# Down projection of a two-layer trunk: 16 of 22 inner tiles by a seven-product scheme, and three reorders

## The chip, the cores and the metric

The kernel runs on one core of a Trainium2 chip. What counts is the device time of one execution in microseconds (us); a measured version is given as the median of its executions, and the profile is of one execution taken by itself.

## The reference

One step of a streaming encoder: 1024 prompt tokens and 32 sample tokens, 1056 in all (`T`), with a model width of 1024, through two layers. Layer 0 mixes tokens by gated linear attention, layer 1 by latent attention with 8 heads; each layer ends with the same channel mixer, which is what most of the change is about:

```python
def conv_glu(h, prev, w_in, conv_w, conv_b, w_out):
    g, u = jnp.split(h @ w_in, [D_FF], axis=-1)
    gc, new_prev = causal_dwconv(g, prev, conv_w, conv_b)
    return (jax.nn.gelu(gc, approximate=False) * u) @ w_out, new_prev
...
x = x + o
h = rmsnorm(x, norm_ffn[l])
o, prev = conv_glu(h, ffn_prev0[l], w_ffn_in[l], ffn_conv_w[l], ffn_conv_b[l], w_ffn_out[l])
x = x + o
```

`D_FF` is 2816, the causal convolution has three taps, and everything is float32.

## The kernel before

**Precision.** Each float32 product of matrices is made of three products of rounded numbers: a factor is split into a rounded part (`hi`, an ACT copy to `F32R`) and the rest (`lo`, a subtraction on DVE or POOL), and the products hi by hi, lo by hi and hi by lo are summed in PSUM. The lines are 341 to 343 (`mm3`) for plain products and 758 to 760 (`product`) for the seven-product scheme. Every operand that PE uses thus costs an ACT copy and a subtraction first.

**Layout.** Features lie on the 128 partitions. The residual stream `xT` is 8 tiles of 128 features by 1056 tokens. The inner width 2816 is 22 tiles of 128 (`NF`). All large loads and stores are issued by SP on one hardware queue (`wraw`, two slots for weights; `s_a`, `s_x`, DRAM scratch).

**First half of the mixer, `pe_unit_ffn`.** For each inner tile the gate rows and the up rows are to be computed for all tokens: a 2 by 2 problem (gate and up rows; left and right 528 tokens; lower and upper half of the 1024 features). Tile 0 is done plainly, the tiles 1 to 21 (called units here) with seven products in place of eight: P1 P2 P6 P5 P7 P4 P3. A product is 4 pieces of 128 features by 3 matmuls by 2 halves of 264 columns, 24 matmuls; a unit is 168 matmuls. The sums that the scheme needs are made of weights by `s_sums` (DVE, four subtractions or additions of 128x512) and of activations once per layer by `t_sum` (T1 to T4). PSUM results leave through ACT copies (`snap`, three in a unit) and DVE additions of 128x528 (`gate_left`, `up_right`, `up_left`, `gate_right`). Then DVE runs the convolution (`conv`, lines 1076 to 1093), ACT the GELU (`gelu`), DVE the product with the up rows (`glu`), and SP stores the tile to `s_a` (`sp_a_out`).

**Second half, `pe_down_first` and `pe_down_ffn`.** 11 groups of 2 inner tiles. A group multiplies 2 by 128 rows of `w_ffn_out` with its two activation tiles for 8 output tiles and 3 chunks of 352 tokens: 8 x 3 x 2 x 3 = 144 matmuls of 352 columns. DVE adds each of the 24 results of 128x352 to `xT` (L585; in the first group L1153, which reads the residual stream back through `xback`). For each group SP reloads two `s_a` tiles (`sp_a_in`), ACT rounds them (L935, L939) and POOL makes the rest (L1193, L1195).

**What sets the order.** Nothing is scheduled by a program: each engine has its own list, written out by hand (`pe_ffn`, `act_ffn`, `dve_ffn`, `pool_ffn`, `sp_ffn`), and waits on counting semaphores where another engine's result or a free buffer is needed. An instruction that waits holds back everything behind it on its engine. SP's list at the end of the units is driven by PE's product counter `prod`: one load or store after each product.

**The other places.** For the second tile, `snap(2, 0)` copies P1 into the gate buffer `fg[0]`, which `conv(0)` still reads, so ACT waits for the convolution of tile 0:

```python
                if n == 0:
                    act.wait_ge(S("row_zeros"), layer + 1)
                    act.wait_ge(S("conv"), NF * layer + f - 1)
                    state_in(f)
```

In the latent attention, `head_split(act, 0)` (L2405) rounds the first head's keys `akraw`, after a load has brought them, and stands in ACT's list right behind the rounding of the last keys and ahead of the copies of the last query tiles (L2080, L2085). In the attention steps, DVE adds two blocks of the output projection to `xT` in each step (`add(s, 0)` and `add(s, 1)`, L585); the second stands behind the reciprocal and the scaling of the softmax rows (L2507, L2509).

## Time and profile before

| | |
|---|---|
| median of 3 executions | 2638.41 us (2638.26 to 2638.42) |
| the profiled execution, its own time | 2640.56 us |
| its span, first to last instruction | 2638.7 us |
| PE busy | 2579.3 us (98%) |
| DVE / ACT / POOL busy | 1487.2 / 1000.7 / 932.6 us (56 / 38 / 35%) |
| mean granted TensorE clock | 0.995 |
| DMA | 221.93 MB, mean 84 GB/s |

The span is 1.9 us shorter than the profiled execution's own time, and that is 2.1 us above the median. PE is the matmul engine; its busy time includes the overlapping tails of matmuls, so what a matmul costs is read from the distance between two starts. "Idle before" in a row is the time in which an engine waited before that instruction, and the arrow names what ended the wait.

### The profile page before, as it was taken

What the parts mean: (1) busy time and instruction counts of PE and PEld (TensorE: products, weight loads), DVE (VectorE), ACT (ScalarE), POOL (GpSimd) and SP (SyncE); (2) the same over time, 40 slices, a digit from 0 to 9 for tenths busy, and PEclk for the clock granted to TensorE, in tenths of its full rate; (3) what the DMA queues carried; (4) which work ended last, traced back from release to release, by engine and by line L of the source; (5) the groups of instructions that cost most, each with busy time, mean ns of one, the idle gap of its engine ahead of it and who ended that gap; (6) DMA issues with size and microseconds to landing.
All of it is one profiled execution on the core that took longest, in us unless ns stands there. A gap on an engine that the chain in (4) does not pass through costs nothing.

```text
span 2638.7 us, 43372 instructions
## 1 busy us (share of the span) xinstructions
PE 2579.3 (98%) x18206; PEld 2500.3 (95%) x18206; DVE 1487.2 (56%) x2660; ACT 1000.7 (38%) x1651; POOL 932.6 (35%) x546
## 2 busy tenths in 40 slices
PE   8999999999999999999999989999999999999999
PEld 7999999999999999999998988889999999999999
DVE  6735353578555455555625875555696555446554
ACT  6333333364233322111547756444453233321111
POOL 5121212152433444444522223223334433444441
PEclk9999999999999999999999999999999999999999
DMA  3111111122222224222213253132122222233222
GB/s 110 35 37 35 37 39 34 38 98 81 81 74 90 74 81 180 74 98 98 70 45 126 108 198 124 49 98 73 61 71 82 81 73 89 74 136 117 98 98 100
DMA packets 182159, 221.93 MB, mean 84 GB/s; under 512 B 16690, under 2 KB 145344, under 8 KB 181328
## 3 DMA queue, kind: packets, MB, share of 16 engines
q1 hardware_dynamic: 179567, 217.08, 24.5%
q8 instruction: 144, 2.36, 0.4%
q10 hardware_dynamic: 2400, 2.10, 0.3%
q14 instruction: 48, 0.39, 0.0%
HBM read 160.56 MB, written 58.59 MB: 83 GB/s over the span
## 4 chain that ended last, share of the span: by engine, by line
PE 89%; DVE 6%; ACT 2%; issue 1%; DMA 1%; SPq 0%; POOL 0%; DVEq 0%; ACTq 0%; POOLq 0%
PE ps L341 14%; PE ps L343 13%; PE ps L342 13%; PE ps L758 11%; PE ps L760 11%; PE ps L759 11%; PE ps L2366 3%; PE ps L1289 1%; PE ps L2350 1%; PE ps L1276 1%; PE ps L1277 1%; PE ps L1278 1%; DVE xT L585 1%; PE ps L1365 1%; PE ps L1348 1%
## 5 line engine op out<-in xcount | busy, mean ns | idle before, releaser
L585 DVE TENSOR_TENSOR xT<-xT,ps 128x352 f32<-128x352 f32 x672 | 347.2, 519 | 249.2 <-PE ps L343 248.1
L1170 POOL TENSOR_TENSOR wlo<-wraw,whi 128x1024 fp32r<-128x1024 f32 x78 | 187.3, 2401 | 454.7 <-DVE s_raw L993 454.7
L306 POOL TENSOR_TENSOR wlo<-wraw,whi 128x2048 fp32r<-128x2048 f32 (+1 forms) x37 | 168.3, 4550 | 498.2 <-ACT whi L299 468.8
L341 PE MATMUL ps<-fahi,whi 128*128 128x352 f32 x960 | 311.1, 324 | 0.1
L343 PE MATMUL ps<-fahi,wlo 128*128 128x352 f32 x960 | 308.1, 321 | 0.0
L342 PE MATMUL ps<-falo,whi 128*128 128x352 f32 x960 | 307.9, 321 | 0.0
L299 ACT ACTIVATE whi<-wraw 128x2048 fp32r<-128x2048 f32 x40 | 76.6, 1914 | 396.7 <-DMA wraw<-w_ffn_out 328.1
L341 PE MATMUL ps<-hh,whi 128*128 128x352 f32 x648 | 218.5, 337 | 0.6 <-ACT cqr L2679 0.3
L343 PE MATMUL ps<-hh,wlo 128*128 128x352 f32 x648 | 208.2, 321 | 0.0
L342 PE MATMUL ps<-hl,whi 128*128 128x352 f32 x648 | 207.9, 321 | 0.0
L758 PE MATMUL ps<-hh,whi 128*128 128x264 f32 x672 | 191.5, 285 | 0.4 <-DVE wlo L1019 0.4
L759 PE MATMUL ps<-hl,whi 128*128 128x264 f32 x672 | 191.2, 285 | 0.0
L760 PE MATMUL ps<-hh,wlo 128*128 128x264 f32 x672 | 191.2, 284 | 0.0
L341 PEld LDWEIGHTS ps<-fahi,whi 128*128 128x128 f32 x960 | 180.1, 188 | 0.9 <-DVE xT L585 0.4
L342 PEld LDWEIGHTS ps<-falo,whi 128*128 128x128 f32 x960 | 180.4, 188 | 0.2
L343 PEld LDWEIGHTS ps<-fahi,wlo 128*128 128x128 f32 x960 | 180.3, 188 | 0.0
L1170 POOL TENSOR_TENSOR s_lo<-s_raw,s_hi 128x512 fp32r<-128x512 f32 x80 | 148.4, 1855 | 60.0 <-ACT s_hi L890 60.0
L1047 DVE TENSOR_TENSOR hf<-hf,ps 128x528 f32<-128x528 f32 x42 | 29.6, 704 | 188.6 <-ACT hf L926 188.6
L758 PEld LDWEIGHTS ps<-hh,whi 128*128 128x128 f32 x672 | 126.5, 188 | 1.3 <-DVE wlo L1019 0.8
L341 PEld LDWEIGHTS ps<-hh,whi 128*128 128x128 f32 x648 | 121.6, 188 | 5.7 <-issue 2.6
L760 PEld LDWEIGHTS ps<-hh,wlo 128*128 128x128 f32 x672 | 126.6, 188 | 0.0
L759 PEld LDWEIGHTS ps<-hl,whi 128*128 128x128 f32 x672 | 126.4, 188 | 0.0
(414 smaller groups left out, 7920.0 us busy)
## 6 DMA issues: line engine op xcount, KB each, us to landing
wraw<-w_ffn_in SPq DMA_DIRECT2D x88, 512.0 KB, 3.8
s_a<-hf SPq DMA_DIRECT2D x44, 528.0 KB, 3.3
wraw<-w_ffn_out SPq DMA_DIRECT2D x44, 512.0 KB, 4.3
fa<-s_a SPq DMA_DIRECT2D x40, 528.0 KB, 6.1
...
```

The costliest lines, as they stand in the source:

```text
L299: act.activation(hi[:, 0:cols], raw[:, 0:cols], ACT.Copy).then_inc(S("w_hi"), 1)
L306: pool.tensor_tensor(lo[:, 0:cols], raw[:, 0:cols], hi[:, 0:cols].bitcast(F32), ALU.subtract).then_inc(S("w_lo"), 1)
L341: nc.tensor.matmul(out, w[0], x[0], start=start, stop=False)
L342: nc.tensor.matmul(out, w[0], x[1], start=False, stop=False)
L343: return nc.tensor.matmul(out, w[1], x[0], start=False, stop=stop)
L585: dve.tensor_tensor(xT[:, m, tc(j)], xT[:, m, tc(j)], ps[:, banks[i % len(banks)], 0:TC], ALU.add)\
L758: nc.tensor.matmul(out, w_[0], x_[0], start=first, stop=False, skip_group_check=True)
L759: nc.tensor.matmul(out, w_[0], x_[1], start=False, stop=False, skip_group_check=True)
L760: last = nc.tensor.matmul(out, w_[1], x_[0], start=False, stop=(k == HK - 1), skip_group_check=True)
L1047: dve.tensor_tensor(right, left, two(U_SIDE), ALU.add).then_inc(S("summed"), 1)
L1170: return pool.tensor_tensor(lo[:, cols], raw[:, cols], hi[:, cols].bitcast(F32), ALU.subtract)
L2366: last = pe.matmul(ps[:, 6, 0:m], av[h % 2][0:n, kk0 // P, :], aPT[s % 2][0:n, i, 0:m], start=(i == 0), stop=(i == len(tiles) - 1))
```

## The change

The down projection of the inner tiles 1 to 16 moves to the seven-product scheme. Two parts of 8 inner tiles, four pairs of output tiles in each: `ND` = 8 more units per layer (numbers 22 to 29, `pe_unit_down`), each again 7 products of 24 matmuls of 264 columns. The 2 by 2 problem is now: two output tiles of a pair; odd and even inner tiles (X11 and X21 on the left 528 tokens, X22 on the right); left and right tokens. The six inner tiles that are left (0, 17 to 21) make `NG2` = 3 groups of the old kind.

What comes with it: the activation sums T1 to T4 are made tile pair by tile pair on DVE while the units 3 to 17 run (`pair_sum`, four of 128x528 in each odd unit), stored to a new scratch `s_t` (`sp_t_out`, 8 stores of 1.08 MB), and reloaded in blocks of 1.08 MB, seven for each part (`sp_block`), which ACT rounds (`block_hi`, 128x2112) and DVE (five of seven) or POOL (T3 and X22) splits (`block_lo`). The weights of a unit are a 512 KB load for each of two halves (`sp_down_w`); their sums S2, S3, S4 go into space freed in other buffers (`side`), S4 of an even unit into the rows of the last even activation tile and of an odd unit into those of the last odd one, so the sum waits for that tile's store. `into_x` adds PSUM results of 128x528 to `xT`, seven in a unit; `xT` is reloaded from `s_x` in four loads of 1.08 MB (`sp_x_in`).

The three reorders: `snap(2, 0)` goes to a buffer of its own (`first_left`), and the wait on the first convolution moves to `snap(2, 1)` and `gate_left(2)`; `head_split(act, 0)` moves behind the copies of the last query tiles; in steps with 32 rows (`STEPS[s][1] == NG`) the second addition to `xT` comes before the reciprocal.

The core of the diff:

```diff
+ND = 8
...
+        first_left = h32[:, 0, TH:T]
...
+        PAIRS = ((3, 4), (0, 1), (2, 5), (6, 7))
...
+        def side(n, f):
+
+            cols = slice(TH, TH + QB)
+            if n == "S3" and f % 2:
+                return fcr[:, QB:2 * QB], fc[:, 0:QB], fcr[:, 0:QB]
+            if n == "S4":
+                at_ = (2 * (f % 2) + 1) * T + TH
+                return hh[:, 2 * (f % 2), cols], hf32[:, at_:at_ + QB], hh[:, 2 * (f % 2) + 1, cols]
+            r_ = 0 if n == "S2" else 2
+            return hl[:, r_, cols], h32[:, r_ + 1, cols], hl[:, r_ + 1, cols]
+
...
+        def sp_block(sp, layer, part, i):
+
+            name, n = BLOCKS[part][i], 7 * part + i
+            if A_LOADS * layer + n >= 2:
+                before, count = load_count(layer, n - 2)
+                sp.wait_ge(S(before), nth(before, count))
+            if name[0] == "T":
+                sp.wait_ge(S("t_stored"), nth("t_stored", 16 * (NT * layer + 4 * part + 4)))
+                src = A["s_t"][4 * part:4 * part + 4, :, ("T1", "T3", "T2", "T4").index(name), :].rearrange("q p t -> p q t")
+            else:
+                odd = name == "X11"
+                sp.wait_ge(S(f"a_stored{int(odd)}"), nth(f"a_stored{int(odd)}", 16 * (NFG * layer + 4 * part + 4 + (not odd))))
+                first, t0 = ND * part + (1 if odd else 2), TH if name == "X22" else 0
+                src = A["s_a"][first:first + ND - 1:2, :, t0:t0 + TH].rearrange("q p t -> p q t")
+            sem, _ = load_count(layer, n)
+            sp.dma_start(xblock(name)[1], src).then_inc(S(sem), 16)
...
+        def sp_x_in(sp, layer, p):
+
+            sem = f"x_back{p % 2}"
+            if p >= 2:
+                sp.wait_ge(S(sem), nth(sem, 16 * (2 * layer + 1)))
+            m0, m1 = PAIRS[p]
+            rows = slice(m0, m1 + 1, m1 - m0)
+            sp.dma_start(xT[:, rows, :], A["s_x"][:, rows, :]).then_inc(S(sem), 16)
...
-            sp_a_in(sp, layer, 0)
+            sp_block(sp, layer, 0, 0)
+            prod(f, 2)
+            sp_block(sp, layer, 0, 1)
+            sp_next_w(sp, layer, c0, f + 2, 0)
+            sp_x_in(sp, layer, 0)
             prod(f, 3)
-            sp.dma_start(xback[0][:, :, :], A["s_x"][:, 0:HK, :]).then_inc(S("x_back0"), 16)
+            sp_block(sp, layer, 0, 2)
             sp_a_out(sp, layer, f - 1)
-            prod(f, 4)
-            sp_a_in(sp, layer, 1)
-            prod(f, 5)
-            sp.dma_start(xback[1][:, :, :], A["s_x"][:, HK:KD, :]).then_inc(S("x_back1"), 16)
-            prod(f, 6)
-            sp_w_out(sp, layer, c0, 1)
+            for n in (4, 5, 6):
+                prod(f, n)
+                sp_block(sp, layer, 0, n - 1)
+            sp_next_w(sp, layer, c0, f + 2, 1)
+            prod(f, 7)
+            sp_block(sp, layer, 0, 6)
+            sp_x_in(sp, layer, 1)
+            sp.wait_ge(S("conv"), NF * layer + NF - 1)
+            sp_x_in(sp, layer, 2)
+            for f in range(NF, NF + ND):
+                last = f == NF + ND - 1
+                for n in range(1, 8):
+                    if n in (2, 7) or f == NF + 3 or last and n in (3, 4):
+                        prod(f, n)
+                    if f == NF + 3:
+                        sp_block(sp, layer, 1, n - 1)
+                    if last and n in (3, 4):
+                        sp_a_in(sp, layer, n - 3)
+                    if n in (2, 7):
+                        sp_next_w(sp, layer, c0, f + 2, n // 7)
+                if f == NF:
+                    sp.wait_ge(S("conv"), NF * (layer + 1))
+                    sp_x_in(sp, layer, 3)
+                    sp_a_out(sp, layer, NF - 1)
             sp_a_in(sp, layer, 2)
-            sp_a_out(sp, layer, f)
-            for g in range(2, NFG):
-                sp.wait_ge(S("down_mm"), 24 * (b0 + g - 1))
-                sp_w_out(sp, layer, c0, g)
-                if g > 2:
-                    sp_a_in(sp, layer, g)
+            sp.wait_ge(S("down_mm"), 24 * (b0 + 1))
+            for kk in range(2):
+                sp_w_out(sp, layer, c0, 2, kk)
...
+            def p7():
+                low_pool(1)
+                pe.wait_ge(S("s_lo"), cnt("s_lo", layer, f, 3))
+                pe.wait_ge(S("summed"), cnt("summed", layer, f, 3))
+                product(a, w_extra("S3"), x_in("T3"), True).then_inc(S("prod"), 1)
+
+            def p3():
+                low_pool(2)
+                pe.wait_ge(S("s_lo"), cnt("s_lo", layer, f, 4))
+                pe.wait_ge(S("summed"), cnt("summed", layer, f, 4))
+                product(U_SIDE, w_extra("S4"), x_in("X22"), True).then_inc(S("prod"), 1)
...
+                act.wait_ge(S("prod"), cnt("prod", layer, f, ORDER(f).index(("P1", "P6", "P7")[n]) + 1))
+                if n == (1 if f == 2 else 0):
...
+                if (f, n) == (2, 0):
+                    dst = first_left
...
+            def refill(part, f, early, late):
+
+                block_hi(part, 0)
+                early()
+                block_hi(part, 1)
+                side_hi(f, "S2")
+                late()
+                block_hi(part, 2)
+                block_hi(part, 3)
+                w_hi_side(f)
+                block_hi(part, 4)
+                side_hi(f, "S3")
+                side_hi(f, "S4")
+                block_hi(part, 5)
+                block_hi(part, 6)
...
+                if f in (NF, NF + 1):
+                    stored = f"a_stored{f % 2}"
+                    dve.wait_ge(S(stored), nth(stored, 16 * NFG * (layer + 1)))
                 dve.tensor_tensor(s4, w[1], s2, ALU.subtract).then_inc(S("s_sum"), 1)
...
+                if f == NF - 1:
+                    w_low_in(f + 1)
+                    block_lo(0, 0)
+                    block_lo(0, 1)
+                pair = (f - 3) // 2 if f % 2 and f <= 2 * NT + 1 else None
+                if pair is not None:
+                    pair_sum(pair, "T1")
+                    pair_sum(pair, "T3")
+                up_right(f)
+                if f == NF - 1:
...
+            for f in range(NF, NF + ND):
+                part, first, more = (f - NF) // 4, (f - NF) % 4 == 0, f + 1 < NF + ND
+                side_lo(f, "S2")
+                if first:
+                    into_x(f, 1)
+                    block_lo(part, 3)
+                w_low_side(f)
+                if not first:
+                    into_x(f, 1)
+                side_lo(f, "S3")
+                if f == NF:
+                    conv(NF - 1)
+                into_x(f, 2)
+                if f > NF:
+                    side_lo(f, "S4")
+                into_x(f, 3)
+                if f == NF:
+                    side_lo(f, "S4")
+                if first:
+                    into_x(f, 4)
+                    block_lo(part, BLOCKS[part].index("T4"))
+                    if f == NF:
+                        glu(NF - 1)
+                    into_x(f, 5)
                     s_sums(f + 1)
-                up_right(f)
-                up_left(f)
-                gate_right(f)
-                conv(f)
-
-            before = 24 * b0
...
+            for part in range(2):
+                for name in ("T3", "X22"):
+                    block_lo(part, name)
...
+                early = s < NS and STEPS[s][1] == NG
+                if early:
+                    add(s, 1)
...
-                if PREP[u] == (MP - 1, "ks", 1, 3):
+                if PREP[u] == (MP - 1, "q", 0, 2):
                     head_split(act, 0)
-                if PREP[u] == (MP - 1, "q", 0, 2):
                     q_split(act, 0)
```

**First place, SP's queue at the end of the units** (layer 0). Before, from the reload of the first group's tiles (`h_52<-s_a`) on; the number behind a name is that of the buffer, and `z_mm` is the name of the counter that `prod` uses, `x_loaded0` and `x_loaded1` those of the stores of even and odd tiles:

```order
L668 DMA h_52<-s_a 128x2x528 [waits x_loaded1,x_loaded0,z_mm]
L668 DMA h_52<-s_a 128x2x528
L717 DMA xback_130<-s_x 128x4224 [waits z_mm]
L661 DMA s_a<-hf_219 256x1x528 [waits glu]
L671 DMA fa_137<-s_a 128x1056 [waits x_loaded1,x_loaded0,z_mm]
L671 DMA fa_137<-s_a 128x1056
L722 DMA xback_131<-s_x 128x4224 [waits z_mm]
```

Now, from the first block (X11) to the store of tile 21:

```order
L741 DMA h_52<-s_a 128x4x528 [waits x_loaded1,z_mm]
L741 DMA h_52<-s_a 128x4x528 [waits x_loaded0,z_mm]
L332 DMA wraw_55<-w_ffn_out 128x8x128
L759 DMA xT<-s_x 128x2112
L741 DMA hflat<-s_t 128x4x528 [waits consts,x_loaded2,z_mm]
L720 DMA s_a<-hf_220 256x1x528 [waits glu]
...
L332 DMA wraw_56<-w_ffn_out 128x8x128 [waits z_mm] x2
L759 DMA xT<-s_x 128x2112 [waits consts_late,conv]
L720 DMA s_a<-hf_220 256x1x528 [waits glu]
```

The store of tile 20 (the first `s_a<-hf_220`) has four loads ahead of it that were not there, and that of tile 21 (the last row) follows a weight load and a load of `xT`.

**Second place, DVE in unit 21** (layer 0). Before:

```order
L1042 TENSOR_TENSOR fg_111<-fg_111,ps 128x528 [waits z_mm,z_ln]
L1101 TENSOR_TENSOR hf_219<-hf_219,fc 128x2x528 [waits gelu]
L1047 TENSOR_TENSOR hf_219<-hf_219,ps 128x528 [waits z_ln]
L1053 TENSOR_TENSOR hf_219<-hf_219,ps 128x528 [waits z_min,z_mm]
L1065 TENSOR_TENSOR fg_111<-fg_111,ps 128x528 [waits z_mm]
```

Now:

```order
L1266 TENSOR_TENSOR fg_111<-fg_111,ps 128x528 [waits z_mm,z_ln]
L1325 TENSOR_TENSOR hf_220<-hf_220,fc 128x2x528 [waits gelu]
L1192 TENSOR_TENSOR h_52<-wraw_56 128x512 [waits consts,w_loaded1]
L1194 TENSOR_TENSOR wraw_56<-wraw_56 128x4x128 [waits z_scan]
L1196 TENSOR_TENSOR h_52<-wraw_56 128x512 [waits z_scan]
L1201 TENSOR_TENSOR hf_220<-wraw_56,h_52 128x512 [waits x_loaded0,z_scan]
L1242 TENSOR_TENSOR wlo_58<-wraw_56,whi_54 128x1024 [waits z_scan,w_hi]
L1331 TENSOR_TENSOR hl<-h_52,hh 128x4x528 [waits b_exp] x2
L1271 TENSOR_TENSOR hf_220<-hf_220,ps 128x528 [waits z_ln]
L1331 TENSOR_TENSOR T2lo<-hflat,T2hi 128x2112 [waits b_exp]
```

Between the product with the up rows (L1325) and `up_right(21)` (L1271), for which PE's last product waits, there are now the four weight sums of unit 22, the last with the wait on the store of tile 20, and three subtractions.

**Third place, ACT ahead of the attention**, before:

```order
L2096 ACTIVATE ksq<-ksq 128x1568 [waits unit_act]
L2405 ACTIVATE akh_181<-akraw_185 128x1568 [waits head_loaded0]
L2080 ACTIVATE qw<-ps 128x352 [waits q_left,normed,unit_mm]
L2085 ACTIVATE sqh_164<-ps 128x352 [waits unit_mm]
L2080 ACTIVATE qw<-ps 128x352 [waits unit_mm]
```

Now:

```order
L2403 ACTIVATE ksq<-ksq 128x1568 [waits unit_act]
L2387 ACTIVATE qw<-ps 128x352 [waits q_left,normed,unit_mm]
L2392 ACTIVATE sqh_166<-ps 128x352 [waits unit_mm]
...
L2392 ACTIVATE sqh_166<-ps 128x352 [waits unit_mm]
L2712 ACTIVATE akh_183<-akraw_187 128x1568 [waits head_loaded0]
```

The rounding of the keys, with its wait on a load, moved from ahead of six PSUM copies to behind them.

## Rows read from the trace of the kernel before

**Rows 1.** The page's busy times over the whole span

```profile
PE 2579.3 (98%) x18206; PEld 2500.3 (95%) x18206; DVE 1487.2 (56%) x2660; ACT 1000.7 (38%) x1651; POOL 932.6 (35%) x546
```

**Rows 2.** Windows: length, busy (instructions) of the five engines, clock, DMA share, GB/s

```profile
700.00:800.00 100.00, 100.00 (x825) 100.00 (x824) 52.03 (x85) 32.02 (x40) 39.74 (x20) 1.00 0.25 81
```

**Rows 3.** By source line: ns minimum/median/maximum, first and last start (groups 1 and 2 for PE)

```profile
L1065 DVE TENSOR_TENSOR fg<-fg,ps x19: 704/705/706, 662.2 to 1029.6; 128x528 f32<-128x528 f32 x19
...
L342 PE MATMUL ps<-falo,whi x48: 318/322/324, 1052.6 to 1075.0; 128*128 128x352 f32 x48
...
L341 PE MATMUL ps<-hhf,whi x48: 321/323/326, 1029.4 to 1052.0; 128*128 128x352 f32 x48
```

**Rows 4.** By source line: the sums, roundings and splits that the change repeats

```profile
L989 DVE TENSOR_TENSOR wraw<-wraw 128x512 f32<-128x512 f32 x15 | 10.4, 693 | 0.5
...
L1015 DVE TENSOR_TENSOR T2lo<-hflat,T2hi x2: 2345/2347/2349, 599.8 to 1944.6; 128x2112 fp32r<-128x2112 f32 x2
...
L1019 DVE TENSOR_TENSOR wlo<-wraw,whi x2: 1218/1222/1226, 602.1 to 613.6; 128x1024 fp32r<-128x1024 f32 x2
...
L935 ACT ACTIVATE hhf<-h x2: 1959/1959/1959, 1018.5 to 2363.3; 128x2112 fp32r<-128x2112 f32 x2
...
L1195 POOL TENSOR_TENSOR falo<-fa,fahi x10: 4742/4760/4781, 1045.7 to 1247.6; 128x2112 fp32r<-128x2112 f32 x10
```

**Rows 5.** SP's timeline, the landing times of stores (L661), and a window

```profile
1017.97 0.34 SPq L717 DMA_DIRECT2D xback<-s_x  x1
1018.35 0.56 SPq L661 DMA_DIRECT2D s_a<-hf  x1
...
DMA to landing us min/median/max: 3.1/3.3/9.3
...
1030.00:1040.00 10.00, 10.00 (x65) 10.00 (x64) 9.66 (x20) 1.97 (x2) 0.00 (x0) 1.00 1.00 416
```

**Rows 6.** Timelines of DVE and POOL: start, duration, instruction, wait before

```profile
619.43 3.27 DVE L1083 SCALAR_TENSOR_TENSOR fc<-fg,par,fc 128x1024 f32<-128x1024 f32 x1
...
640.76 1.28 DVE L1083 SCALAR_TENSOR_TENSOR fc<-fg,par,fc 128x1024 f32<-128x1024 f32 x1
...
658.16 0.70 DVE L1047 TENSOR_TENSOR hf<-hf,ps 128x528 f32<-128x528 f32 x1 [3.00 <-ACT hf L926]
...
618.79 2.83 POOL L1170 TENSOR_TENSOR s_lo<-s_raw,s_hi 128x1024 fp32r<-128x1024 f32 x1
...
657.66 1.30 POOL L1170 TENSOR_TENSOR s_lo<-s_raw,s_hi 128x512 fp32r<-128x512 f32 x1
```

**Rows 7.** PE's waits: total us, times, longest us

```profile
PE ps L341 <- DVE xT L585: 10.4, 25, 1.3
PE ps L758 <- ACT fg L926: 8.6, 2, 4.3
```

**Rows 8.** Timelines of PE and ACT at unit 2, and a window

```profile
625.33 0.56 PE L758 MATMUL ps<-T2hi,s_hi 128*128 128x264 f32 x1 [4.32 <-ACT fg L926]
...
629.60 0.29 PE L758 MATMUL ps<-T1hi,whi 128*128 128x264 f32 x1
...
624.59 0.59 ACT L926 ACTIVATE fg<-ps 128x528 f32<-128x528 f32 x1
...
625.00:630.00 5.00, 4.67 (x28) 4.70 (x29) 3.06 (x4) 3.70 (x5) 0.00 (x0) 0.69 0.01 3
```

**Rows 9.** Timelines of ACT and PE ahead of the attention

```profile
1559.17 1.51 ACT L2405 ACTIVATE akh<-akraw 128x1568 fp32r<-128x1568 f32 x1 [4.77 <-DMA apraw<-s_p]
...
1563.55 0.63 PE L2050 MATMUL ps<-sqh,ones_r 128*128 128x352 f32 x1 [5.03 <-DVE qsl L2109]
```

**Rows 10.** Timelines of DVE and PE at a step with 32 rows

```profile
1667.25 0.70 DVE L2509 TENSOR_SCALAR aP<-aP,rl 32x544 f32<-32x544 f32 x1
1667.88 0.50 DVE L585 TENSOR_TENSOR xT<-xT,ps 128x352 f32<-128x352 f32 x1
...
1668.44 0.43 PE L341 MATMUL ps<-oh,moh 128*128 128x352 f32 x1 [0.87 <-DVE xT L585]
```

More of the change, by code:

```diff
@@ L763, in pe_unit_ffn @@
         def pe_unit_ffn(pe, layer, c, f):
-            u = unit_no(layer, f)
             slot = c[0]
@@ new lines, in s_sums @@
+                s2, s3, s4 = [v.rearrange("p (k n) -> p k n", k=HK) for v in (
+                    [raw[:, n * QB:(n + 1) * QB] for n in range(3)] if f < NF else
+                    [side(n, f)[1] for n in ("S2", "S3", "S4")])]
+                dve.wait_ge(S(f"w_loaded{slot}"), 32 * loads)
+                if 2 < f < NF:
+                    dve.wait_ge(S("prod"), cnt("prod", layer, f - 1, 0))
+                if f == NF:
+                    dve.wait_ge(S("t_stored"), nth("t_stored", 16 * NT * (layer + 1)))
@@ L2510, in dve_att @@
                                       None, ALU.mult).then_inc(S("probs"), 1)
-                add(s, 1)
+                if not early:
+                    add(s, 1)
             down_norm_dve(dve, fill_before(MP - 1), 3, 3, R_FFN + KD,
```

459 lines of the change are left out of this document (300 added, 159 removed).

## Prediction, written before the run

> **What bounds the kernel now.** I read the busy times first, then windows, the waits of PE, and timelines where PE waits. PE is busy 98% of the span [rows 1]. In a window of the units PE has 825 matmuls in 100 us without a gap at clock 1.00, while DVE is busy 52%, POOL 40%, ACT 32% and the DMA share is 0.25 [rows 2]: there matmul time is the bound, and the other engines have room on average. PE waits little, most for additions to `xT` (10.4 us in 25 waits) and for ACT's copy `fg` (8.6 us in 2) [rows 7]. So what saves matmuls shortens the kernel, and what makes PE wait lengthens it in full. All sums below are against the profiled execution (2640.6); the median is 2.2 lower, which I take off at the end.
>
> **The change, part by part.**
>
> *1. Matmuls.* The last addition of a unit (L1065) starts at 662.2 the first time and at 1029.6 the nineteenth: 18 periods, 20.41 us each [rows 3], so 121.5 ns for each of 168 matmuls and 2.915 us for a product. In the first down group the 48 matmuls of L341 start from 1029.4 to 1052.0, 47 steps in 22.6, so the group takes 23.1; in the second L342 gives 47 steps in 22.4, 22.9 [rows 3]. I take 23.0 for a group of 144, 159.7 ns for a matmul. A group and a unit replace each other one for one, eight per layer: 8 x (23.0 - 20.41) = 20.7, **-41 us** for both layers (ends: 22.9 and 23.1, -40 and -43).
>
> *2. Pair sums* (four additions of 128x528 in each odd unit). One costs 0.70 to 0.72 by the row of such an addition [rows 3]. DVE has 48% idle in the units [rows 2]; T1 and T3 end before `up_right` is needed by PE's next product but one, and the convolution ends 1.6 later, still ahead of the next snapshot. Cost 0; the upper bound is 1 us in each of 16 units if POOL holds them up. The stores to `s_t` are 8 x 1.08 MB beside a DMA share of 0.25: 0.
>
> *3. First refill (units 21 to 23), the largest term.* I worked out the timeline of all engines step by step from their lists. t = 0 is the start of unit 21's first product; product n of it ends at 2.915 n.
> What SP's queue does: a store alone lands in 3.3 us; the one issued 0.4 behind a load of 2.16 MB lands in 9.3 [rows 5]. At 0.41 MB per us (416 GB/s at a DMA share of 1.00, rows 5) the 0.54 MB of a store are 1.3, so some 1.9 are fixed. Served in order of issue, load and store end 1.9 + 2.70/0.41 = 8.5 after the load's issue; measured are 9.7. So the store does stand behind the load, and the 1.2 more go to the upper end. The Trainium skill ("DMA: Bandwidth & Descriptors", Queues, rings and completion order) also says that each DMA engine consumes descriptors in ring order; by that rule, the trace agrees.
> (a) The store of tile 20 is issued at t = 9.5, after product 3. Ahead of it in the queue stand block 1, a weight half (0.52 MB), a load of `xT` (1.08) and block 2; block 0, issued at 3.2, is through at 7.7. So 7.7 + (1.08 + 0.52 + 1.08 + 1.08 + 0.54)/0.41 = 18.2, with the completion 18.6. On DVE the fourth sum of unit 22 waits for it. Behind it stand that sum 0.7, a split of 1024 1.2, two splits of 2112 at 2.35 each [rows 4], and only then `up_right(21)` 0.7: 18.6 + 7.3 = 25.9. PE wants it for the seventh product at 17.5: **8.5 us**.
> (b) Unit 22: P7 waits for the `xT` addition behind the last convolution (1.5), and POOL's two splits of 4.76 [rows 4] hold DVE's (P3 1.8, P4 1.2): **4.5 us**.
> (c) The store of tile 21 is issued behind unit 22's last product, a weight half and the last load of `xT`: 1.9 + 2.14/0.41 and some issue time = 7.2 after the product's end; then a sum 0.7, an addition 0.7, a split 1.2, and only then P1 of unit 23: **10 us**.
> The blocking used in (b): L1083 took 3.27 at 619.43 while POOL ran 618.79 to 621.62, against 1.28 alone, and an addition out of PSUM ran in its usual 0.70 beside a POOL instruction [rows 6]. So POOL holds up DVE instructions with two SBUF operands, not those with PSUM.
> (d) Clock: after a stall of 4.32 us the product took 625.33 to 629.60 = 4.27 in place of 2.915, with granted clock 0.69 in 625:630 [rows 8]: part of it ran at the lower level (1.2 GHz). I add 1.4 to 1.7 for each of the stalls (a), (c): **3.2**.
>
> *4. Second refill (unit 26).* Loads start three products early and are in time. DVE's split of the fourth block and `side_lo` wait behind POOL's T3 and X22: P6 2.4 and P5 4.6, with the clock 1.5 more: **8.5 us**. If POOL didn't hold DVE, 0.
>
> *5. Units 23 to 25, 27 to 29, three groups.* About 20 DVE instructions of 0.6 to 1.2, some 15 us in 20.4: hidden, 0 to 0.2.
> Sum of 3 to 5: 8.5 + 4.5 + 10 + 3.2 + 8.5 + 0.2 = 35 per layer; with a DMA rate of 0.39 it is 36.4. I take 36, **+72**. Ends: 33 and 40 per layer.
>
> *6. Second tile's snapshot.* PE waits 4.32 us at 625.33, and 8.6 in both layers [rows 7, 8], plus 1.4 each of clock. P6 could begin at 620.85. But P7 then waits for `snap(2, 1)`, which stands behind the convolution and a GELU (0.6). And the weight sums of unit 3 stand on DVE behind the first product with the up rows and start as before, so POOL's splits do too, and DVE's second convolution, held by them (its long step at 640.76, rows 6), moves little; `up_left(2)` stands behind it, and P2 of unit 3 waits for that. I get P2 of unit 3 some 1.7 earlier per layer. **-3.4**; ends 0 and -11.4 (2 x 5.7).
>
> *7. First keys.* ACT's L2405 waited 4.77 us for a load, the query copies behind it came late, and PE idled 5.03 at 1563.55 [rows 9]. Moved: the copies start when PE has their sums, 4 to 5 earlier. L2405 takes 1.51 behind six copies of 0.45, and POOL's split of the keys follows it; the first scores need that only some 15 us later, which covers it. Nothing else is queued behind it that PE needs sooner. **-5.5** with the clock; ends 0 and -6.7.
>
> *8. Rows of 32.* The addition at 1667.88 stands behind a scaling of 0.70, and PE waits 0.87 at 1668.44 [rows 10]; three such waits of about 0.9. **-2.5**; ends 0 and -3.
>
> **Sum.** 2640.6 - 41 + 72 - 3.4 - 5.5 - 2.5 = 2660.2; less 2.2: **2658 us**, 0.7% slower.
>
> **A rule that weighs on 3(b) and 4.** The rows show a DVE instruction held until POOL's was over [rows 6], in one order only: POOL had begun first. The Trainium skill ("SBUF — State Buffer", Who interferes with whom) says that whichever starts first keeps the shared ports for its whole instruction. By it, POOL's splits are held by DVE's as well, where DVE is first; that moves T3 and X22 later and would cost up to 2 us more per layer, 2662 in place of 2658. No row here shows POOL held.
>
> **The rivals.** A measurement of this kernel can tell about 0.2% (5.3 us) from no change.
>
> *A, POOL doesn't hold DVE in the refills* (the splits alternate, DVE finds gaps). Then 3(b) is 1.5 and 4 is 0: 25 per layer, 2588.2 + 50 - 2.2 = **2636**, no change. Against: rows 6. Chance 0.13.
>
> *B, the stores are not behind the loads* (land 3.3 after issue). (a) becomes 2.5, (c) 7.1, part of it returns as waits in unit 22: 29 per layer, **2644**. Against: 9.3 in rows 5. Chance 0.08.
>
> *C, the other side: DVE is in time.* At P3 of unit 21 and P1 of unit 23 PE finds what it needs nearly ready, since stores land as if alone and no DVE instruction is held. What is left is 13 per layer, the time by which the stores are issued late: 2588.2 + 26 - 2.2 = **2612**, 1% faster. It decides from stalls under 23.5 us per layer (2588.2 + 47 - 2.2 = 2633). For it: engines other than PE are half idle [rows 2]. Against: both rows named above. I also leave room for steps that I read too strictly. Chance 0.19.
>
> *D, more waits than I count*: loads of 1.08 MB with rows of 2112 bytes slower than 0.41 MB per us, POOL held too, the keys' reorder worth nothing: 40 per layer and +5.5, **2672**. Chance 0.10.
>
> **Numbers.** Forecast 0.50, own range 2648 to 2668 (ends of 3 and 6 to 8). Faster by over 0.2%: C and a third of A, 0.24. Within: most of A, half of B, 0.12. Slower: 0.64. The range of 8 in 10 reaches up to D's value and down into C: 2618 to 2672.
>
> **What would show it.** Right: PE waiting about 8 us ahead of P3 of unit 21 and about 10 ahead of P1 of unit 23 in each layer, with the clock below 0.9 behind both; the stores of tiles 20 and 21 landing 7 to 9 us after issue; waits of 2 to 5 in unit 26 with DVE instructions stretched beside POOL's of 4.7; matmuls in units 22 to 29 121.5 ns apart; PE's wait at unit 2 under 1; no 5.03 ahead of the query sums. Wrong: total PE waits in the refills under 23 us per layer (then C), stretches without stall but units over 20.5 us (then DVE bounds them).

## The result, and the profile after

The changed kernel takes 2676.40 us (median of 4, 2675.4 to 2678.53) against 2638.41 before: ratio 1.0144, 95% interval 1.0128 to 1.0159, so 38 us slower. The forecast was slower, but by 20 us, and its range ended at 2672. The profiled execution took 2675.52 with a span of 2673.4, so the profile shows 34.7 us of the 38.

The first rows of the page, and the clock from the view of the cores:

```profile
span 2673.4 us, 44342 instructions
PE 2556.9 (96%) x18590; PEld 2477.3 (93%) x18590; DVE 1657.6 (62%) x2616; ACT 1051.2 (39%) x1727; POOL 842.1 (31%) x522
core 0: 2673.4 us, clock 0.983
```

Against [rows 1] PE is busy 22 us less, although the kernel is longer: there are 384 matmuls more, but shorter ones; matmul time was saved, and waits took its place. PE's waits, as total, times, longest:

```profile
PE ps L864 <- DVE wlo L1242: 29.4, 7, 11.3
PE ps L864 <- DVE hf L1271: 22.4, 4, 10.3
PE ps L864 <- DVE xT L1351: 16.0, 4, 5.8
...
PE ps L864 <- DVE hf L1277: 5.0, 2, 2.5
PE ps L345 <- DVE xT L589: 7.2, 19, 1.3
PE ps L345 <- POOL apl L2264: 3.9, 1, 3.9
```

L864 is the first matmul line of a product. The three first rows were not there before: the weight split of the next unit (`w_low_in`), `up_right(21)` and the additions to `xT`. Of the 8.6 us behind `fg` 0.7 are left, and 3.2 of the 10.4 behind `xT` are gone [rows 7], but a wait for `up_left(2)` (L1277) and one for POOL's last split for the first scores (`apl`) are new.

Where the 34.7 us of span are, by distances between the same instructions in both traces:

| stretch | before | after | difference | on record |
|---|---|---|---|---|
| last addition of unit 1 to that of unit 20, both layers | 787.4 | 784.9 | -2.5 | -3.4 |
| unit 20's last addition to the last group's last L341/L345, layer 0 | 275.4 | 299.0 | +23.6 | +15.3 |
| the same, layer 1 | 277.6 | 300.7 | +23.1 | +15.3 |
| last root of the keys to the first scaled step of 768 | 42.4 | 37.0 | -5.4 | -5.5 |
| from there to the last such step | 280.7 | 277.2 | -3.5 | -2.5 |
| all else (from the unrounded distances) | | | -0.5 | 0 |

The pairs of units with and without pair sums take 21.1 and 19.7 us by their last additions, 40.8 together, twice 20.41 [rows 3]: the pair sums are hidden. So the down projection costs 46.7 us where 30.6 were forecast, and the reorders give 11.5 where 11.4 were.

Inside a layer, unit 20's last addition to the first matmul of the groups takes 227.2 us (1006.55 to 1233.73); nine units of 20.41 are 183.7. So 43.5 are lost. PE's timeline (start, duration, matmul, wait before) has five long waits in layer 0, and the same five in layer 1 within 0.1 (the products behind them within 0.3):

```profile
1034.29 0.59 PE L864 MATMUL ps<-hh,s_hi 128*128 128x264 f32 x1 [10.27 <-DVE hf L1271]
...
1057.04 0.56 PE L864 MATMUL ps<-T3hi,hl 128*128 128x264 f32 x1 [5.78 <-DVE xT L1351]
...
1080.02 0.59 PE L864 MATMUL ps<-hh,whi 128*128 128x264 f32 x1 [11.34 <-DVE wlo L1242]
...
1154.83 0.37 PE L864 MATMUL ps<-T1hi,whi 128*128 128x264 f32 x1 [2.97 <-DVE wlo L1242]
...
1161.76 0.46 PE L864 MATMUL ps<-T3hi,hl 128*128 128x264 f32 x1 [2.24 <-DVE xT L1351]
```

| place | wait forecast | wait measured | its product's 24 matmuls over 2.915 us |
|---|---|---|---|
| P3 of unit 21 | 8.5 | 10.3 | 2.2 |
| unit 22: P7 | 1.5 | 5.8 | 2.5 |
| unit 22: P3, P4 | 3.0 | under 0.25 | 0.2, 0.2 |
| P1 of unit 23 | 10 | 11.3 | 1.6 |
| unit 26: P6 | 2.4 | under 0.25 | 0.2 |
| unit 26: P5, P7 | 4.6 | 3.0, 2.2 | 1.8, 1.6 |
| sum | 30 | 32.6 | 10.3 (forecast 4.7) |

The waits come to 32.6 us and the slow products to 10.3, 9.7 of it right behind the five waits; together 42.9 of the 43.5. In windows behind the first, second and third wait the clock (the seventh number, after the busy times) is at its lower level, or for part of the window (0.67):

```profile
1034.00:1037.00 3.00, 2.71 (x12) 2.71 (x13) 3.00 (x3) 3.00 (x4) 2.49 (x1) 0.50 0.72 214
1037.00:1040.00 3.00, 3.00 (x19) 3.00 (x18) 0.51 (x2) 0.33 (x1) 3.00 (x1) 0.67 0.00 0
1057.00:1060.00 3.00, 2.96 (x13) 2.99 (x14) 3.00 (x3) 0.73 (x1) 0.00 (x0) 0.50 0.02 5
1060.00:1063.00 3.00, 3.00 (x16) 3.00 (x15) 1.78 (x3) 0.00 (x0) 0.00 (x0) 0.52 0.00 0
1080.00:1083.00 3.00, 2.98 (x13) 2.98 (x14) 2.31 (x3) 0.00 (x0) 0.00 (x0) 0.50 0.00 0
```

0.50 is 1.2 of 2.4 GHz. And the two links of the first wait, DVE's and SP's timelines:

```profile
1015.32 0.36 SPq L741 DMA_DIRECT2D hflat<-s_t  x1
1015.72 0.83 SPq L720 DMA_DIRECT2D s_a<-hf  x1
...
1015.71 0.69 DVE L1196 TENSOR_TENSOR h<-wraw 128x512 f32<-128x512 f32 x1
1027.06 0.69 DVE L1201 TENSOR_TENSOR hf<-wraw,h 128x512 f32<-128x512 f32 x1 [10.67 <-DMA s_a<-hf]
```

The store of tile 20 is issued at 1015.72 and lands 11.2 us later; before, one behind a single load took 9.3, one alone 3.3 [rows 5]. The fourth weight sum waits for it, and behind that sum and three splits `up_right(21)` releases PE.

The wait ahead of P7 of unit 22 has another cause than the last convolution by itself. POOL's and DVE's timelines there:

```profile
1046.97 4.94 POOL L1493 TENSOR_TENSOR hl<-h,hh 128x2112 fp32r<-128x2112 f32 x1 [5.89 <-ACT hh L1106]
...
1047.24 4.72 DVE L1300 COPY sm<-fg 128x32 f32<-128x32 f32 x1
```

The first instruction of that convolution, a copy of 128x32 with a median of 0.18, begins behind POOL's split of X22 and ends with it, 4.5 us late; the rest of the convolution and the addition that P7 waits for follow it. Layer 1 has the same (4.72).

### The profile page after: what moved, and what is told of

The parts are those of the page before. It is cut to its first block, busy times and chain, and to the rows that moved or that the text cites. A ratio compares the mean times of both kernels' runs of the same rounds, so it can differ in the third digit from the quotient of the medians.

```text
span 2673.4 us, 44342 instructions
## 1 busy us (share of the span) xinstructions
PE 2556.9 (96%) x18590; PEld 2477.3 (93%) x18590; DVE 1657.6 (62%) x2616; ACT 1051.2 (39%) x1727; POOL 842.1 (31%) x522
## 4 chain that ended last, share of the span: by engine, by line
PE 82%; DVE 11%; DMA 2%; issue 2%; ACT 2%; POOL 1%; SPq 1%; DVEq 0%; ACTq 0%; POOLq 0%
PE ps L864 14%; PE ps L866 13%; PE ps L865 13%; PE ps L345 9%; PE ps L347 8%; PE ps L346 8%; PE ps L2673 3%; DMA s_a<-hf 1%; PE ps L1596 1%; PE ps L2657 1%; PE ps L1583 1%; PE ps L1585 1%; PE ps L1584 1%; DVE fc L1307 1%; PE ps L2640 1%
## 5 line engine op out<-in xcount | busy, mean ns | idle before, releaser
L864 PE MATMUL ps<-hh,whi 128*128 128x264 f32 x928 | 266.2, 287 | 28.5 <-DVE wlo L1242 23.4
L589 DVE TENSOR_TENSOR xT<-xT,ps 128x352 f32<-128x352 f32 x336 | 172.2, 518 | 106.3 <-PE ps L347 105.2
L345 PE MATMUL ps<-hh,whi 128*128 128x352 f32 x648 | 218.5, 337 | 0.6 <-ACT cqr L2990 0.3
L310 POOL TENSOR_TENSOR wlo<-wraw,whi 128x2048 fp32r<-128x2048 f32 (+1 forms) x21 | 94.3, 4490 | 367.2 <-ACT whi L303 337.9
L864 PEld LDWEIGHTS ps<-hh,whi 128*128 128x128 f32 x928 | 176.0, 190 | 30.0 <-DVE wlo L1242 24.6
L1351 DVE TENSOR_TENSOR xT<-xT,ps 128x528 f32<-128x528 f32 x112 | 78.2, 701 | 109.1 <-PE ps L866 108.9
L864 PE MATMUL ps<-T1hi,whi 128*128 128x264 f32 x464 | 133.6, 288 | 6.0 <-DVE wlo L1242 5.9
L865 PE MATMUL ps<-T1lo,whi 128*128 128x264 f32 x464 | 133.3, 287 | 0.0
L866 PE MATMUL ps<-T1hi,wlo 128*128 128x264 f32 x464 | 133.0, 287 | 0.0
L864 PE MATMUL ps<-T4hi,whi 128*128 128x264 f32 x464 | 132.0, 284 | 0.0
L865 PE MATMUL ps<-T4lo,whi 128*128 128x264 f32 x464 | 131.9, 284 | 0.0
L866 PE MATMUL ps<-T4hi,wlo 128*128 128x264 f32 x464 | 131.5, 283 | 0.0
L345 PEld LDWEIGHTS ps<-hh,whi 128*128 128x128 f32 x648 | 121.6, 188 | 5.6 <-issue 2.6
```

The source lines that it names most:

```text
L310: pool.tensor_tensor(lo[:, 0:cols], raw[:, 0:cols], hi[:, 0:cols].bitcast(F32), ALU.subtract).then_inc(S("w_lo"), 1)
L345: nc.tensor.matmul(out, w[0], x[0], start=start, stop=False)
L589: dve.tensor_tensor(xT[:, m, tc(j)], xT[:, m, tc(j)], ps[:, banks[i % len(banks)], 0:TC], ALU.add)\
L864: nc.tensor.matmul(out, w_[0], x_[0], start=first, stop=False, skip_group_check=True)
L865: nc.tensor.matmul(out, w_[0], x_[1], start=False, stop=False, skip_group_check=True)
L866: last = nc.tensor.matmul(out, w_[1], x_[0], start=False, stop=(k == HK - 1), skip_group_check=True)
```

## The experiments

Two ideas had to be told apart for each wait: the theory (the wait is that of the store or of a DVE instruction that POOL holds up, as on record) and a rival (blocks late anyway, DVE full anyway). The runs were made on several chips, and the kernel before took 2638.4 to 2642.5 on them (the column "before"); all ratios are to it on the same chip. So a difference of times between two rows with different "before" can be off by some 4 us. "Refill" is the distance of 227.2 above, in layers 0 and 1; it is read inside one trace and is the surer measure.

| run | us | before | ratio (95%) | refill, layers 0 and 1 |
|---|---|---|---|---|
| the change | 2676.4 | 2638.4 | 1.0144 (1.0128 to 1.0159) | 227.2, 226.7 |
| e1_store20 | 2666.9 | 2640.0 | 1.0099 (1.0082 to 1.0116) | 223.3, 222.4 |
| e2_store21 | 2647.7 | 2640.0 | 1.0026 (1.0015 to 1.0037) | 213.4, 213.4 |
| e3_both_stores | 2639.6 | 2640.0 | 0.9994 (0.9985 to 1.0004) | 210.6, 209.8 |
| e4_no_pool | 2657.6 | 2640.0 | 1.0071 (1.0053 to 1.0089) | 218.6, 218.3 |
| e5_stores_no_pool | 2618.1 | 2642.5 | 0.9909 (0.9894 to 0.9924) | 198.2, 196.8 |
| e6_reorders_alone | 2626.8 | 2642.5 | 0.9944 (0.9931 to 0.9958) | |
| e7_filler_matmuls | 2674.3 | 2642.5 | 1.0125 (1.0110 to 1.0141) | 226.7, 226.6 |
| e8_store_queue | 2642.0 | 2639.8 | 1.0013 (1.0003 to 1.0023) | 210.8, 210.2 |
| e9_dve_order | 2616.0 | 2639.8 | 0.9907 (0.9891 to 0.9924) | 196.0, 196.5 |
| e10_loads_order | 2612.5 | 2639.8 | 0.9896 (0.9880 to 0.9913) | 193.6, 195.2 |
| e11_keys_alone | 2636.2 | 2640.2 | 0.9982 (0.9972 to 0.9992) |  |
| e12_rows32_alone | 2634.8 | 2640.2 | 0.9979 (0.9969 to 0.9988) |  |

### The stores of tiles 20 and 21

```diff
             sp_block(sp, layer, 0, 1)
+            sp_a_out(sp, layer, f - 1)      # e1, e3
             sp_next_w(sp, layer, c0, f + 2, 0)
             sp_x_in(sp, layer, 0)
             prod(f, 3)
             sp_block(sp, layer, 0, 2)
-            sp_a_out(sp, layer, f - 1)      # e1, e3
...
                 for n in range(1, 8):
+                    if f == NF and n == 3:              # e2, e3
+                        sp_a_out(sp, layer, NF - 1)
...
                     sp_x_in(sp, layer, 3)
-                    sp_a_out(sp, layer, NF - 1)         # e2, e3
```

> The changed kernel with one DMA moved in SP's list: the store of tile 20 is issued before the weight half, the xT load and block 2 instead of behind them. My theory (DVE's fourth weight sum stands behind that store in the queue, and PE's P3 of unit 21 behind DVE): the store lands at about 12.5 us of unit 21 instead of 20.5, PE's wait ahead of P3 falls from 10.3 to about 2 us in each layer, with 1.5 to 2 us of clock, so 2676 - 16 to 20 = 2656 to 2660. Rival (the blocks themselves come too late, the store only happens to be last): the wait falls by under 3 us and the time stays over 2670.

> The changed kernel with the store of tile 21 issued as soon as its product with the up rows is done, ahead of unit 22's last product, the weight half and the xT load. My theory: the 11.3 us ahead of P1 of unit 23 fall to under 1 and the 1.6 us of clock go with them, 12 to 13 us per layer, 2676 - 25 = 2651. Rival (w_low of unit 23 is late for another reason, such as the rounding of the weights on ACT behind a GELU): under 5 us per layer, over 2666.

> Both store moves together. If the two waits are independent: 2676 - 18 - 25 = 2633, within 4 us. If the time saved at the first only moves the wait to the next transfer (X22 and T4 blocks for unit 22), the sum comes out 5 to 12 us short, 2638 to 2645.

DVE in e1_store20, unit 21:

```profile
1017.62 0.69 DVE L1196 TENSOR_TENSOR h<-wraw 128x512 f32<-128x512 f32 x1
1021.07 0.69 DVE L1201 TENSOR_TENSOR hf<-wraw,h 128x512 f32<-128x512 f32 x1 [2.76 <-DMA s_a<-hf]
1021.87 1.23 DVE L1242 TENSOR_TENSOR wlo<-wraw,whi 128x1024 fp32r<-128x1024 f32 x1
1023.01 4.62 DVE L1331 TENSOR_TENSOR hl<-h,hh 128x2112 fp32r<-128x2112 f32 x2
1027.55 0.70 DVE L1271 TENSOR_TENSOR hf<-hf,ps 128x528 f32<-128x528 f32 x1
```

DVE waits 2.8 us for the store in place of 10.7, and PE 2.4 ahead of P3 in place of 10.3, as the theory had it, with the same work between. But only 3.9 of those 8 us stay in the refill: in unit 22 PE now waits 3.4 us ahead of P5, with a slow product of 4.7 behind it, which it didn't before. The cause is in the timelines of POOL and DVE there:

```profile
1037.47 4.95 POOL L1493 TENSOR_TENSOR T3lo<-hflat,T3hi 128x2112 fp32r<-128x2112 f32 x1 [30.34 <-ACT T3hi L1106]
...
1037.79 5.72 DVE L1242 TENSOR_TENSOR wlo<-wraw,whi 128x1024 fp32r<-128x1024 f32 x1
...
1043.61 0.36 PE L864 MATMUL ps<-T1hi,whi 128*128 128x264 f32 x1 [3.36 <-issue]
```

The weight split, 1.22 in the changed kernel, now falls beside POOL's split of T3 and takes 5.72; P5 starts 0.1 after its end. So the wait was given back through the other cause, not through late blocks, and the rival is out. The total is 9.5 us (12 by the ratios), where 16 to 20 were expected.

The second move gave all that it should: the wait of 11.3 is gone, 28.8 us in total (25 expected), 13.8 in the refill. Together they give 36.8 us, of the 38.3 that they give one by one; so the two waits are independent or nearly so. The 2633 expected for that case was missed because the first move gave 9.5 and not 18.

### Is it the queue, or the engines behind it?

```diff
             sp_block(sp, layer, 0, 2)
-            sp_a_out(sp, layer, f - 1)
...
-                    refill(0, f + 1, lambda: snap(NF - 1, 1), lambda: snap(NF - 1, 2))
+                    refill(0, f + 1, lambda: (sp_a_out(act, layer, NF - 2), snap(NF - 1, 1)), lambda: snap(NF - 1, 2))
...
                 w_hi_in(f)
+                if f == NF + 1:
+                    sp_a_out(act, layer, NF - 1)
```

> The changed kernel with the stores of tiles 20 and 21 issued by ACT on its own queue (behind block 0's rounding, and behind the weights of unit 23), all loads left where they are on SP's. If the stores were late because they stood behind loads in one queue, they land 4 to 6 us after their issue though the loads still run, and the waits ahead of P3 of unit 21 and P1 of unit 23 fall to about 2 and 0 to 1: near e3_both_stores, 2640 to 2646. If the DMA engines' load itself makes them late, whatever the queue, they take 7 to 10 us again and the time stays over 2665.

The total is the one of the first expectation, but for half of its reason. Timelines of ACT's queue and DVE:

```profile
1016.06 0.67 ACTq L720 DMA_DIRECT2D s_a<-hf  x1
...
1025.17 0.69 DVE L1201 TENSOR_TENSOR hf<-wraw,h 128x512 f32<-128x512 f32 x1 [7.71 <-DMA s_a<-hf]
...
DMA to landing us min/median/max: 3.1/6.1/9.0
```

The store of tile 20, on a queue of its own and issued at nearly the same time, still takes 9.0 us (11.2 in SP's queue; in layer 1 9.9 and 11.3), and PE waits 7.3. The second, issued when no load runs, takes 3.1, and its wait is gone. So the first is late because loads are in flight on the same engines (a weight half, `xT` rows and T2, 2.7 MB, all issued within 3 us before it or just after); its place in the queue is worth 2 us. What helped in e1_store20 was to issue it before those loads: there it landed after 4.7. The time doesn't tell the two ways apart here: the refill is 210.8 in e8_store_queue and 210.6 in e3_both_stores, where PE waits 2.5 us ahead of P3 but then 3.0 more ahead of P5 of unit 22.

### POOL beside DVE

```diff
-            for part in range(2):
-                for name in ("T3", "X22"):
-                    block_lo(part, name)        # POOL's list
...
                 side_lo(f, "S3")
+                if first:
+                    block_lo(part, 4)           # T3, DVE's list
...
                 if first:
+                    block_lo(part, BLOCKS[part].index("X22"))
                     into_x(f, 4)
```

> The changed kernel with the splits of T3 and X22 made by DVE (2.35 us each) instead of POOL (4.8), so that nothing on POOL runs beside DVE in the refills. My theory (POOL's instruction keeps DVE out): PE's waits in unit 22 (5.8) and unit 26 (3.0 + 2.2) fall to 0 to 2 and the clock losses behind them (2.5, 1.8, 1.6) mostly go, 7 to 12 us per layer: 2652 to 2662. Rival (DVE is simply full in the refills): 4.7 us more work on DVE makes these waits longer by 2 to 5 per layer, 2680 to 2686.

In the changed kernel, POOL and DVE in unit 26:

```profile
1147.35 6.25 POOL L1493 TENSOR_TENSOR T3lo<-hflat,T3hi 128x2112 fp32r<-128x2112 f32 x1 [95.44 <-ACT T3hi L1106]
1153.57 5.67 POOL L1493 TENSOR_TENSOR hl<-h,hh 128x2112 fp32r<-128x2112 f32 x1
...
1146.67 2.35 DVE L1331 TENSOR_TENSOR T1lo<-hflat,T1hi 128x2112 fp32r<-128x2112 f32 x1
1148.94 5.75 DVE L1242 TENSOR_TENSOR wlo<-wraw,whi 128x1024 fp32r<-128x1024 f32 x1
1154.61 5.17 DVE L1336 TENSOR_TENSOR hl<-h,hl 128x512 fp32r<-128x512 f32 x1
```

and DVE in the same unit of e4_no_pool:

```profile
1144.89 2.35 DVE L1332 TENSOR_TENSOR T1lo<-hflat,T1hi 128x2112 fp32r<-128x2112 f32 x1
1147.16 1.22 DVE L1242 TENSOR_TENSOR wlo<-wraw,whi 128x1024 fp32r<-128x1024 f32 x1
1148.30 0.69 DVE L1337 TENSOR_TENSOR hl<-h,hl 128x512 fp32r<-128x512 f32 x1
1148.90 2.35 DVE L1332 TENSOR_TENSOR T3lo<-hflat,T3hi 128x2112 fp32r<-128x2112 f32 x1
```

A split of 1.22 took 5.75, one of 0.69 took 5.17. It goes both ways: POOL's split, 4.76 by itself [rows 4], takes 6.25 when DVE's T1 split has begun 0.7 before it. That is the rule of the Trainium skill that the prediction weighed ("SBUF — State Buffer", Who interferes with whom): here the trace agrees with it in both directions. In e4_no_pool the copy of 128x32 in unit 22 takes 0.18 again too. With 4.7 us more work on DVE, the refill is 8.6 us shorter; in unit 22 the wait ahead of P7 is 3.5, and in unit 26 no wait over 1.2 us is left. The rival is out.

### The clock

```diff
                     if f == NF - 1:
+                        pe.wait_ge(S("snap"), cnt("snap", layer, f, 3))
+                        filler(U_SUM, hh[:, HK, TH:TH + P], hh[:, HK, TH:TH + HH], 76)
                     pe.wait_ge(S("summed"), cnt("summed", layer, f, 2))
...
                 if f == NF + 1:
                     pe.wait_ge(S("snap"), cnt("snap", layer, NF, 0))
+                    filler(a, hh[:, 0, 0:P], hh[:, 0, 0:HH], 86)
                 pe.wait_ge(S("w_lo"), c[1] + 1)
```

> The changed kernel with unused matmuls in the two long waits: 76 ahead of P3 of unit 21 and 86 ahead of P1 of unit 23 (9.2 and 10.4 us at 121.5 ns), whose results are overwritten. They add nothing to the computation. If the slow products behind these waits (5.12 and 4.52 us in place of 2.915) come from PE having stood still, the products take about 2.95 and the time falls by 2.2 + 1.6 per layer, 2676.4 - 7.6 = 2669. If they come from something else (operands late, DMA traffic), they stay at 4.5 to 5.1 and the time stays at 2676.

PE's row at P3 of unit 21, and the window behind it:

```profile
1033.22 0.39 PE L864 MATMUL ps<-hh,s_hi 128*128 128x264 f32 x1 [0.40 <-DVE hf L1282]
...
1033.00:1036.00 3.00, 2.77 (x23) 2.78 (x24) 3.00 (x3) 3.00 (x4) 1.50 (x1) 1.00 1.05 344
```

With PE busy up to 0.4 us before, the product takes 3.01 in place of 5.12, the clock is 1.00. The filler reached in two of its four places: in layer 1 that was P1 of unit 23 (wait 0.9, product 3.03). In the other two, P1 of unit 23 in layer 0 and P3 of unit 21 in layer 1, it ended 2.6 us too soon, and the products took 4.55 and 4.56. So standing still is the cause. But little of it came back: the refills are 0.5 and 0.1 us shorter, where about 2.1 and 1.4 were taken out (the times, 2.1 us apart and not the 7.6 expected, are of two chips, and their ratios overlap). In layer 0 PE wins 2.8 us in unit 21, and then waits 6.8 in place of 5.8 ahead of P7 of unit 22, since DVE is not faster; and the store of tile 21, issued earlier, took 9.4 us to land in place of 7.7. A slow product is free where PE waits for DVE or a store behind it anyway; the 10.3 us of the table count what PE did, and what the clock alone costs in time is not shown.

### The causes together, and further

```diff
             prod(f, 3)
             sp_block(sp, layer, 0, 2)
+            prod(f, 4)
+            sp_block(sp, layer, 0, 3)           # e10: T1 ahead of xT and of the weights
+            sp_x_in(sp, layer, 0)
...
                 dve.tensor_tensor(s2, w[2], w[0], ALU.subtract).then_inc(S("s_sum"), 1)
+                if f == NF:
+                    block_lo(0, 0)              # e9, e10
...
                 up_right(f)
+                if f == NF - 1:
+                    w_low_in(f + 1)             # e9, e10: from ahead of up_right
+                    block_lo(0, 1)
                 up_left(f)
```

> Both store moves and DVE's splits together: e3_both_stores was 2639.6, and taking POOL out of the refills gave 19 us alone (2676.4 to 2657.6). If the two causes are independent 2621; if DVE, now with 4.7 us more work and without the two long waits that covered it, becomes the limit of unit 22, part of it comes back as waits ahead of P7 and P3: 2625 to 2632. My forecast 2627.

> e5_stores_no_pool (2618.1) with DVE's list in unit 21 in another order: the split of block 0 ahead of the sum that waits for the store, and up_right ahead of the weight split and of block 1's. The wait ahead of P3 of unit 21 (2.3) and the 1.6 of clock behind it should go. If PE's time saved is kept: 2618 - 8 = 2610. If unit 22's chain (conv, splits, into_x on DVE) sets P7 of unit 22 anyway, P7's wait grows from 3.5 to 6 or 7 and under 3 us of the 8 remain: 2615 to 2618. I expect the second, since DVE has no gap from the last of unit 21's work to P7 but for 3.1 us ahead of T2.

> e9_dve_order with SP's list changed as well: T2 and T1 are loaded ahead of the xT rows and of the weights of unit 23, so that DVE's 3.1 us gap ahead of T2 goes. Expected 3 to 4 us per layer less than e9_dve_order if both together free the chain to P7 of unit 22, so 2608 to 2612; no change against it if the gap only moves to T3 or X22, whose blocks land last.

The stores and POOL together give 58.3 us by the times, where 36.8 and 18.8 alone are 55.6; the time is 9 below its forecast of 2627. Over both refills they give 58.8, where 33.5 and 17.0 alone are 50.5. So the two moves don't cover each other, and what e1_store20 lost to POOL comes back: the wait ahead of P5 of unit 22 is gone. e9_dve_order took the wait of 2.3 ahead of P3 away, and P7 of unit 22 waited 4.8 in place of 3.5; the two refills together are 2.6 us shorter, the second of the two cases. By its time (2.1 us, on another chip, ratios 0.9907 and 0.9909) it is not told apart from e5_stores_no_pool. e10_loads_order has the shortest time of all, 3.5 us less again on the same chip and 3.7 over both refills; its ratio's interval and that of e9_dve_order overlap, so by the time that step alone isn't shown, and it is half of the 3 to 4 per layer expected. In e10_loads_order DVE has no gap before P7, where e9_dve_order had one of 2.0 ahead of T2:

```profile
1034.76 1.22 DVE L1247 TENSOR_TENSOR wlo<-wraw,whi 128x1024 fp32r<-128x1024 f32 x1
1035.89 0.68 DVE L1342 TENSOR_TENSOR hl<-h,hl 128x512 fp32r<-128x512 f32 x1
1036.49 2.35 DVE L1337 TENSOR_TENSOR T3lo<-hflat,T3hi 128x2112 fp32r<-128x2112 f32 x1
...
1042.57 1.31 DVE L1357 TENSOR_TENSOR xT<-xT,ps 128x528 f32<-128x528 f32 x2
...
1044.02 0.36 PE L867 MATMUL ps<-T3hi,hl 128*128 128x264 f32 x1 [3.50 <-DVE xT L1357]
```

There DVE is the bound. The refill is 193.6, 9.9 us over nine units, and the kernel is 1.04% faster than before (interval 0.87 to 1.20%).

### The reorders alone

e6_reorders_alone is the kernel before with the three reorders, e11_keys_alone and e12_rows32_alone with one each; the edits are those of the diff above.

> The kernel before with the three reorders alone, no part of the down projection's change. From the stretches of the two traces: 1.3 us in each layer for the second tile's snapshot, 4.5 for the first keys, 3.5 for the rows of 32, so 2638.4 - 10.6 = 2628. By the sum on record (3.4, 5.5, 2.5) it would be 2627 as well, so the profile is read by stretch to tell them apart. Rival (part of the 5.4 us ahead of the attention comes from the changed kernel's other timing): 2631 to 2634.

> The kernel before with the reorder of the first keys alone. In e6_reorders_alone the stretch from the last keys' square root to the first scaled step of the attention went from 42.4 to 35.8 us and the attention steps behind it from 280.7 to 275.2. If the keys' reorder acts only ahead of the attention, 2639.8 - 6.5 = 2633 and the attention steps stay at 280.7. If it also takes waits out of the first attention steps, these come down by 2 to 3 us and the time is near 2630.

> The kernel before with the addition moved ahead of the reciprocal in the steps with 32 rows alone. If its worth is the three or so waits of 0.9 us that I read, 2639.8 - 2.5 = 2637 and the attention steps take 278. If all of the 5.5 us of e6_reorders_alone's attention steps are its own, because there is such a step for each of the 8 heads, 2634 and 275.2.

| | before | e6, all three | e11, keys | e12, rows of 32 |
|---|---|---|---|---|
| keys' root to the first scaled step of 768 | 42.4 | 35.8 | 35.8 | 40.6 |
| to the last such step | 280.7 | 275.2 | 280.1 | 276.3 |

The keys' reorder gives 6.6 us ahead of the attention and 0.6 in it, so it acts ahead of it. By its time it gives 4 to 5 us (ratio 0.9982), less than its stretch says. A stretch of one execution is not surer than about 2 us here: in e12_rows32_alone the first row is 1.8 shorter too, although the first step with 32 rows comes only behind it. The new wait for `apl` belongs to this reorder; PE and POOL in e11_keys_alone:

```profile
1576.15 0.41 PE L341 MATMUL ps<-akh,aqh 128*128 128x128 f32 x1 [3.94 <-POOL apl L1957]
...
1572.16 3.85 POOL L1957 TENSOR_TENSOR apl<-apraw,aph 128x264 fp32r<-128x264 f32 x4
```

POOL's splits for the first head run one behind the other (`akl`, `aql`, `apl`), and the first scores now stand ready before the last of them.

The rows of 32 give 4.4 us in the steps. Six of PE's waits for `xT` are gone (25 to 19, 10.4 to 7.2 us in total): the three of about 0.9 that the prediction counted and three of under 0.2, 3.2 us together; what the rest of the 4.4 is stays open. All three reorders give 0.56% (0.42 to 0.69), 15 us, against 11.4 on record, which the interval includes.

## Why the prediction was wrong

The direction and the chain were right, the size was not: +20 forecast, +38 measured.

- *Matmuls (-41).* Right: units 22 to 29 have their products 2.92 apart and 20.41 per unit where nothing waits. Eight groups were 183.4 by the traces (22.9 each, the lower of the two values that the prediction averaged), so the gain is 20.1 per layer, 40.2.
- *Pair sums (0).* Right.
- *First refill, (a) and (c).* The two waits were named with their places and causes, 8.5 and 10 us for 10.3 and 11.3. The store of tile 20 took 11.2 us to land where the sum had 9.1; the 1.2 us that rows 5 had shown over the sum, left to the upper end, belonged into it. And its cause was put too simply: by e8_store_queue the loads in flight count for more than the queue's order.
- *(b) and item 4.* 11.5 forecast, 11.0 measured, but at other products, so the sum is right partly by luck: P7 of unit 22 took all of its unit's wait, P6 of unit 26 none. The prediction had POOL hold up splits, and P7 late by the convolution alone (1.5); POOL held up the convolution's first copy (0.18 became 4.72). That copy has one operand in SBUF, so the prediction's reading of [rows 6], that it is DVE instructions with two such operands, was too narrow.
- *(d), the clock: the step that failed.* The prediction took one row (4.27 for 2.915 behind a wait of 4.3) and charged it to three waits per layer, 4.7 us. Measured are 1.6 to 2.5 us behind each of five waits, those of 2.2 and 3.0 us among them, and with three products 0.2 longer 10.3 per layer: 11 us of the 18 that were missing, the largest part in this account. Waits were 2.6 per layer more than forecast, 5 us; the smaller gain of the matmuls is 1 and the difference of profile and median 3, less the 2 by which the 36 taken lay above the sum of its terms. This is an account of what PE did: by e7_filler_matmuls most of the clock loss taken out came back as waits, so how much of the missing time a faster clock would have saved stays open. No row of before showed the product behind a longer wait; the term should have been bounded upwards by a whole product at half speed, 2.9, for each wait.
- *The reorders (-11.4).* -11.5 in the change, by -2.5, -5.4 and -3.5. What is late next was right for the snapshot: `up_left(2)` with 2.5 us each [rows 8 had 4.3]. For the keys one overlap was wrong: the 15 us that were to cover the splits for the first scores did not, and PE waits 3.9 us there for `apl`; the -5.5 came out all the same.
- *Rivals.* A and B are out: POOL holds DVE up (e4_no_pool), and the stores land late. C (faster, DVE in time) didn't come, but its point of decision is borne out: it put no change at 23.5 us lost per layer, and e5_stores_no_pool, with 14.5 and 13.1 lost in the two layers, is faster. D was near in time (2672). Of its grounds the first two are seen (the store later than 0.41 MB per us gives, POOL held too), the third is not (the keys' reorder gave its share), and the clock, the largest part, it didn't have.
